# Layer borders taken one tile of 128 tokens at a time, and first feed-forward chunks with tokens on partitions

## The reference

```python
for layer in range(2):
    h = rms_norm(x, norm_mix_pre[layer])
    h = neighbourhood_attention(h, ...) if layer == 0 else dilated_attention(h, ...)
    x = x + rms_norm(h, norm_mix_post[layer])
    h = rms_norm(x, norm_ffn_pre[layer])
    x = x + rms_norm((silu(h @ w_gate) * (h @ w_up)) @ w_down, norm_ffn_post[layer])
for l in range(2):
    x = x + 0.5 * swiglu(rms_norm(x, ffn1_norm[l]), ...)
    x = x + hybrid_mixing(rms_norm(x, mix_norm[l]), ...) @ w_out[l]
    x = x + 0.5 * swiglu(rms_norm(x, ffn2_norm[l]), ...)
```

## Time and profile before

| | us |
|---|---|
| median of three runs (lowest, highest) | 1888.59 (1888.42, 1890.96) |
| the profiled execution's own time | 1888.44 |
| its span, first to last instruction | 1886.4 |
| TensorE matmuls busy | 1835.0 |
| VectorE, ScalarE, POOL busy | 1123.6, 899.5, 84.4 |
| HBM traffic over the span | 166 GB/s |
| mean granted clock of TensorE | 0.992 |

### The profile page before, as it was taken

One profiled execution on the slowest core, in us unless ns is written; L12 is line 12 of the kernel. 1 busy time (PEld: TensorE's weight loads), 2 busy tenths in 40 slices (PEclk: granted clock), 3 DMA queues, 4 the chain that ended last, 5 costly groups with the idle time before them and its releaser, 6 DMA issues.

```text
span 1886.4 us, 29866 instructions
## 1 busy us (share of the span) xinstructions
PE 1835.0 (97%) x12748; PEld 1682.5 (89%) x12748; DVE 1123.6 (60%) x1452; ACT 899.5 (48%) x1180; POOL 84.4 (4%) x157
## 2 busy tenths in 40 slices
PE   8989999899999899989999999999999999999999
PEld 6879998689998899889988888999899988889997
DVE  4765664446666566546654766665466547576663
ACT  5645443544444544444444654544454446445442
POOL 0000000202220000000000100000000001000000
PEclk9999999999999999999999999999999999999999
DMA  8433555453333355535554424545445544344452
GB/s 355 146 113 137 187 220 185 145 198 135 135 135 135 113 189 190 215 120 185 189 208 145 146 100 157 179 183 213 163 179 179 207 162 156 112 157 157 179 206 85
DMA packets 45091, 315.90 MB, mean 167 GB/s; under 512 B 5008, under 2 KB 5264, under 8 KB 7840
## 3 DMA queue, kind: packets, MB, share of 16 engines
q1 hardware_dynamic: 44928, 313.98, 45.8%
q0 software_dynamic: 32, 0.03, 0.0%
HBM read 312.94 MB, written 1.05 MB: 166 GB/s over the span
## 4 chain that ended last, share of the span: by engine, by line
PE 90%; DVE 4%; ACT 3%; issue 1%; POOL 1%; DMA 0%; SPq 0%; DVEq 0%; ACTq 0%
PE P L372 88%; DVE wl L1434 1%; ACT wh L983 1%; PE P L533 1%; PE P L385 1%; DVE hcv L1765 0%; DVE xl L1457 0%; ACT xh L1014 0%; POOL hsm L2048 0%; POOL nw L2001 0%; DVE hSS L1797 0%; ACT fs L1076 0%; DVE fg L1543 0%; DVE hxb L1760 0%; DVE rb L1466 0%
## 5 line engine op out<-in xcount | busy, mean ns | idle before, releaser
L1434 DVE TENSOR_TENSOR wl<-raw,wh 128x2048 fp32r<-128x2048 f32 x291 | 665.1, 2289 | 274.2 <-ACT wh L983 273.0
L372 PE MATMUL P<-xh,wh 128*128 128x256 f32 x2896 | 723.2, 287 | 8.3 <-DVE xl L1457 6.2
L372 PE MATMUL P<-xl,wh 128*128 128x256 f32 x2896 | 714.9, 284 | 0.0
L983 ACT ACTIVATE wh<-raw 128x2048 fp32r<-128x2048 f32 x291 | 553.1, 1902 | 238.3 <-PE P L372 231.3
L372 PEld LDWEIGHTS P<-xh,wh 128*128 128x128 f32 x2896 | 558.1, 193 | 19.8 <-issue 15.2
L372 PEld LDWEIGHTS P<-xl,wh 128*128 128x128 f32 x2896 | 558.5, 193 | 0.3
L372 PE MATMUL P<-xh,wl 128*128 128x256 f32 x2896 | 413.6, 284 | 1.9 <-DVE wl L1434 1.2
L372 PEld LDWEIGHTS P<-xh,wl 128*128 128x128 f32 x2896 | 376.9, 192 | 3.5 <-DVE wl L1434 3.5
L372 PE MATMUL P<-wh,fhl 128*128 128x512 f32 x528 | 207.9, 394 | 0.0
L372 PE MATMUL P<-wl,fhh 128*128 128x512 f32 x528 | 206.6, 391 | 0.0
L372 PE MATMUL P<-wh,fhh 128*128 128x512 f32 x528 | 205.7, 390 | 0.0
(11 more groups left out here) (289 smaller groups left out, 1349.5 us busy)
## 6 DMA issues: line engine op xcount, KB each, us to landing
raw<-w_all SPq DMA_DIRECT2D x290, 1024.0 KB, 4.8
nB<-rpb SPq DMA_DIRECT2D x4, 768.0 KB, 16.4
xs<-x_in SPq DMA_DIRECT2D x4, 256.0 KB, 5.1
fgb<-post SPq DMA_DIRECT2D x2, 512.0 KB, 6.3
raw<-w_all SPq DMA_DIRECT2D x2, 512.0 KB, 3.6
out<-xs SPq DMA_DIRECT2D x4, 256.0 KB, 2.1
C<-cst SPq DMA_DIRECT2D x1, 769.0 KB, 13.1
ngb<-post SPq DMA_DIRECT2D x1, 512.0 KB, 6.1
```

The costliest lines, as they stand in the source:

```text
L372: return t_.on.matmul(o, l, r, start=start, stop=stop, skip_group_check=True)
L983: a.on.activation(wh[k][:, 0:w], raw[r][:, 0:w], ACT.Copy).then_inc(*hi.up((m,)))
L1434: v.on.tensor_tensor(wl[k][:, 0:w], raw[r][:, 0:w], wh[k][:, 0:w].bitcast(F32), ALU.subtract).then_inc(*lo.up(m))
```

## The change

All borders are taken by tiles. `half` gets a parameter `split`: the last `split` pieces are used for tile 0 and then again for tile 1 (2 after the attentions, 3 after feed-forwards with post-norm, 1 elsewhere), and signals each tile. Post-norm, residual, `turn` (now 4 transposes of one tile t and one half q of the features), `xh` and `xl` (now 128 columns an instruction) are done tile by tile. The next step starts on tile 0 alone: `values_first` in the attentions and `gates_first` in steps 1, 3 and 4 use their first three pieces for tile 0, then for tile 1, with tile 1's turns between (`border`). In those three feed-forwards the first four chunks are computed with tokens on partitions, in two banks of gate and two of up; Silu and product follow per tile (`fth`), then 8 transposes (`gates_turn`, after chunk 4) bring them to the layout of the rest. The dilated attention keeps its tokens in their own order in `xh`; its second and third value projections read `xh` with a step of two tokens, and the q and k of all groups are put in order (even, odd) as they are read from PSUM. x is fetched tile 0 first. Below, 12 spaces of indentation are cut.

The plan of weight pieces and the constants:

```diff
 DOWN = [(k, h) for h in range(2) for k in range(NF)]
-LAST = [(k, 0) for k in range(6)] + [(k, 1) for k in range(4)] + [(6, 0), (7, 0)] + [(k, 1) for k in range(4, 8)]
+LAST = ([(k, 0) for k in range(6)] + [(k, 1) for k in range(2)] + [(k, 1) for k in range(2, 6)] +
+        [(6, 0), (7, 0), (6, 1), (7, 1)])
...
+        if tok:
+            for name in (g, u):
+                wide(name, layer, 8, 0, 512)
+        for j in range(4 if tok else 0, NF):
             out.append(("P", (g, layer, j * 128), (u, layer, j * 128)))
         halves(d, layer, DOWN)
...
-XBANK = {0: 6, 2: 7, 4: 6, 6: 7}
+TOK_FIRST = (1, 3, 4)
+BORDER = {1: (7, 9), 2: (3, 4), 3: (7, 9), 4: (7, 9)}
```

TensorE's program:

```diff
+def block(s, m, i, c, t, banks, names=(), perm=False):
...
+        o = P[b][:, :]
+        if c == 0:
+            claim(b)
+        mul(o, xa, h3[:, i, halfs(hf)], c == 0, False)
+        t_.wait_ge(*(lo.of(m, i) if m == 0 else lo.of(m)))
+        mul(o, xa, l3[:, i, halfs(hf)], False, False)
+        for z in ((0, 1) if perm else (t,)):
+            t_.wait_ge(*vx.of("lo", s, z, c))
+        k = mul(o, xb, h3[:, i, halfs(hf)], False, c == NK - 1)
+    if names:
+        k.then_inc(*mm.up(*names))
...
+def values_first(s, banks, start=None):
+    m = BASE[s]
+    for t in range(2):
+        for p in range(3):
+            for i in range(2):
+                block(s, m + p, i, 2 * p + i, t, banks[t], [("piece", m + p)] if t and i else ())
+                if t == 0:
+                    border(s, 2 * p + i)
+    tok(s, m + 3, 6, banks)
+def border(s, n):
+    if s and n == BORDER[s][0]:
+        turn(s, 1, 0)
+    if s and n == BORDER[s][1]:
+        turn(s, 1, 1)
+    if s == 0 and n == 1:
+        turn(0, 1, 0)
+        turn(0, 1, 1)
+def gates_first(s):
+    m = BASE[s]
+    place = [(0, 0), (0, 4), (1, 0), (1, 4)]
+    banks = ((0, 1), (2, 4))
+    def part(p, t):
+        g, c0 = place[p]
+        for i in range(4):
+            names = [("tok", s, g, t)] if p % 2 and i == 3 else []
+            if t and i == 3:
+                names.append(("piece", m + p))
+            block(s, m + p, i, c0 + i, t, (banks[g][t],), names)
+            if t == 0:
+                border(s, 4 * p + i)
+    for t in range(2):
+        for p in range(3):
+            part(p, t)
+    for t in range(2):
+        part(3, t)
+        held[banks[0][t]] = [(af, "ts", s, t)]
+        held[banks[1][t]] = [(vf, "th", s, t)]
...
+    whole = len(order) - 4 * split
...
+            if t == 1 and i % 4 == 3:
+                done.append(("piece", n))
...
-        m += 1
+    for i in range(whole):
+        rows(i, (0, 1))
+        after(i, 2)
+    for t in range(2):
+        for i in range(whole, len(order)):
+            rows(i, (t,))
+            after(i, t)
     for t in range(2):
...
+        if s in POST:
+            if t == 1 and i == 37:
+                turn(s + 1, 0, 0)
+            if t == 1 and i == 40:
+                turn(s + 1, 0, 1)
+        elif s < 9:
+            if i == 27:
+                turn(s + 1, 0, 0)
+                turn(s + 1, 1, 0)
+            if t == 1 and i == 41:
+                turn(s + 1, 0, 1)
...
+    if t == 1 and i == 13:
+        turn(s + 1, 0, 0)
+    if t == 1 and i == 15:
+        turn(s + 1, 0, 1)
...
-            next_turn(s)
+        if t == 0 and i == 14:
+            turn(s + 1, 0, 0)
+            turn(s + 1, 1, 0)
+        if t == 1 and i == 13:
+            turn(s + 1, 0, 1)
```

ScalarE's program (a.on):

```diff
+def post_end(s, banks):
+    m = BASE[s + 1]
+    if s in TOK_FIRST:
+        post_squares(s, 1, 0, banks)
+    else:
+        ahead(m)
+        post_squares(s, 0, 0, banks)
+        post_squares(s, 1, 0, banks)
+    post_root(s, 0)
+    ahead(m if s in TOK_FIRST else m + 1)
+    turn(s + 1, 0, 0)
+    turn(s + 1, 0, 1)
+    ahead(m + 1)
+    if s not in TOK_FIRST:
+        post_squares(s, 0, 1, banks)
+    post_squares(s, 1, 1, banks)
+    post_root(s, 1)
+    ahead(m + 2)
+    turn(s + 1, 1, 0)
+    turn(s + 1, 1, 1)
+    all_squares(s + 1)
...
+def add_end(s):
+    turn(s + 1, 0, 1)
+    squares(s + 1, 1, 0)
...
-    turn(0, 0)
-    turn(0, 2)
+    turn(0, 0, 0)
+    turn(0, 0, 1)
+    ahead(0)
+    turn(0, 1, 0)
+    turn(0, 1, 1)
     ahead(2)
-    turn(0, 4)
```

VectorE's program (v.on):

```diff
+def turn(s, t, q):
...
-        n = slice(j * S, (j + 1) * S)
-        k = v.on.scalar_tensor_tensor(lv[:, n], P[b][:, n], par(name, l, c + j), hv[:, n].bitcast(F32), ALU.mult,
-                                      ALU.subtract)
-    k.then_inc(*vx.up(("lo", s, c)))
-def factors(s):
+    v.wait_ge(*ax.of("hi", s, t, 4 * q + 3))
+    for j in range(4):
+        c = 4 * q + j
+        v.on.scalar_tensor_tensor(xl[:, c, toks(t)], P[b][:, toks(j)], par(name, l, c),
+                                  xh[:, c, toks(t)].bitcast(F32), ALU.mult,
+                                  ALU.subtract).then_inc(*vx.up(("lo", s, t, c)))
...
+def add(s, hf, t, banks, scale):
+    v.wait_ge(*mm.of("half", s, hf, t))
+    v.on.scalar_tensor_tensor(xs[:, t, halfs(hf)], P[banks[2 * hf + t]][:, :], scale, xs[:, t, halfs(hf)],
+                              ALU.mult, ALU.add).then_inc(*vx.up(("x", s, hf, t), ("free", s, hf, t)))
...
+def add_end(s, banks, scale):
+    add(s, 1, 0, banks, scale)
+    if s < 9:
+        turn(s + 1, 0, 1)
+    add(s, 1, 1, banks, scale)
...
+    v.wait_ge(*ax.of("psq", s, 1, t))
+    v.wait_ge(*vx.of("pre", s, t))
+    v.on.scalar_tensor_tensor(vv, ss[:, 10 + t:11 + t], 1.0 / D, ss[:, 12 + t:13 + t], ALU.mult,
+                              ALU.add).then_inc(*vx.up(("pv", s, t)))
+    gained(s, 1, t, gb, tmp, banks)
...
+    v.wait_ge(*ax.of("proot", s, t))
...
+def post_end(s, gb, tmp, banks):
+    m = BASE[s + 1]
+    if s not in TOK_FIRST:
+        ahead(m)
+        post_first(s, 0, gb, tmp, banks)
+    post_tile(s, 0, gb, tmp, banks)
+    ahead(m if s in TOK_FIRST else m + 1)
+    turn(s + 1, 0, 0)
+    turn(s + 1, 0, 1)
+    ahead(m + 1)
+    if s not in TOK_FIRST:
+        post_first(s, 1, gb, tmp, banks)
+    post_tile(s, 1, gb, tmp, banks)
+    ahead(m + 2)
+    turn(s + 1, 1, 0)
+    turn(s + 1, 1, 1)
...
 def na():
-    turn(0, 0)
-    turn(0, 2)
-    ahead(2)
-    turn(0, 4)
-    turn(0, 6)
-    for m in range(1, 4):
-        ahead(m + 2)
+    turn(0, 0, 0)
+    turn(0, 0, 1)
+    ahead(0)
...
-                               ALU.mult).then_inc(*va.up(("q", 2, f, z)))
+            qk, b = AD["dq"][:, (f % 3) * 3 + z, :], (3 * f + z) % 2
+            if z:
+                o = qk.rearrange("p (a t j) -> p a t j", a=2, t=2)
+                i = P[b][:, :].rearrange("p (a j t) -> p a t j", a=2, t=2)
+                r = far(rb[:, :]).unsqueeze(1).broadcast_to([128, 2, 2, 128])
+                v.on.tensor_tensor(o, i, r, ALU.mult).then_inc(*va.up(("q", 2, f, z)))
+            else:
+                v.on.tensor_tensor(near(qk[:, 0:S]), far(P[b][:, 0:S]), far(rb[:, :]), ALU.mult)
+                v.on.tensor_tensor(qk[:, S:2 * S], P[b][:, S:2 * S], rb[:, :],
+                                   ALU.mult).then_inc(*va.up(("q", 2, f, z)))
...
-    add(s, 0, banks, 1.0)
+    add_half(s, banks, 1.0)
     ahead(m + 20)
-    next_turn(s)
-    add(s, 1, banks, 1.0)
+    for t in range(2):
+        turn(s + 1, t, 0)
+    add_end(s, banks, 1.0)
```

More of the change, by code:

```diff
@@ new lines, in block, with tok @@
+                if names:
+                    k.then_inc(*mm.up(*names))
+            def tok(s, m, k0, banks, between=None, perm=False):
+                step = 4 // len(banks[0])
+                for i in range(step):
+                    for t in range(2):
+                        block(s, m, i, k0 + i, t, banks[t], [("piece", m)] if t and i == step - 1 else (), perm)
+                    if between is not None and i % 2 and k0 + i < NK - 1:
+                        between()
+            def values_first(s, banks, start=None):
[7 more added lines that the diff above has]
+                tok(s, m + 3, 6, banks)
@@ new lines, in half, with rows @@
+            def half(s, m, order, opnd, ready, banks, split, after):
+                last = {hf: max(i for i in range(len(order)) if order[i][1] == hf) for hf in range(2)}
+                first = {hf: min(i for i in range(len(order)) if order[i][1] == hf) for hf in range(2)}
+                whole = len(order) - 4 * split
+                def rows(i, ts):
+                    c, hf = order[i]
+                    n = m + i // 4
+                    ah_, al_ = opnd(c)
+                    t_.wait_ge(*hi.of(n))
+                    t_.wait_ge(*ready(c)[0])
+                    for t in ts:
+                        b = banks[2 * hf + t]
+                        o = P[b][:, :]
+                        if i == first[hf]:
+                            claim(b)
+                        mul(o, ah_[:, toks(t)], wh[n % RING][:, halfs(i % 4)], i == first[hf], False)
+                        t_.wait_ge(*lo.of(n))
+                        mul(o, ah_[:, toks(t)], wl[n % RING][:, halfs(i % 4)], False, False)
+                        t_.wait_ge(*ready(c)[1])
```

(28 more changed lines are left out.)

551 lines of the change are left out of this document (242 added, 309 removed).

## The result

The kernel after takes **1894.21 us** (median of 13 executions, 1890.96 to 1899.21), the kernel before 1888.79 beside it (13, 1887.19 to 1890.96): a ratio of **1.0028**, 95% interval 1.0019 to 1.0037. That is 5.4 us more, inside the range of 1880 to 1898 and 5.3 us over the forecast of 1888.9, so it falls just outside "no change". The profiled execution has a span of 1892.1 us.

The account below looks back on a forecast made before the run. TensorE was taken as the bound, its matmuls filling 97% of the span, so only its idle or slowed time counts. Terms -18.6 - 1.0 - 0.6 + 9.4 + 7.8 + 3.5 = +0.5 gave 1888.9 us, range 1880 to 1898.

Parts of the forecast that it names:

- (a): At the start, piece 1 is split behind tile 1's work: values 6.9 us later plus 2.5 of clock, +9.4 us.
- chunks: Chunks with tokens on partitions in three feed-forwards, fewer but wider matmuls plus 8 transposes: -0.3 us each, -1.0.
- (b): Out of the hybrids (5 to 6, 8 to 9), TensorE waits for tile 0's late addition: +3.9 us each, +7.8.
- (c): Out of feed-forwards without post-norm (4, 6, 7), TensorE waits 1.15 us for tile 0's addition: +3.5 us.
- The four borders: Borders behind post-norms (0 to 1 through 3 to 4): 35.1 us of idle and slow clock become 16.5 of stalls, gain 18.6.
- piece m+2: At the four borders, its `wl` comes behind tile 1's post-norm on VectorE: TensorE stalls 1.9 us each.
- Strided reads: Values 2 and 3 of the dilated attention, 192 loads with a step of two floats: taken as 0, upper 31 us.
- rival 1: Faster: the clock does not fall at the start and hybrids, 1882.4 us, or 1875 with m+2 stalls hidden; chance 0.31.
- Rival 2: Slower: late `wl` of m+2 makes the clock fall again at each of the four borders, 1897 us; chance 0.22.
- Rival 3: Slower: the strided loads in the dilated attention show, 1898 to 1919 us; chance 0.09.
- The slower side: Slower than before by over 0.2%, through Rival 2 or Rival 3: chance 0.22 + 0.09 = 0.31.

Follow-up runs that it names:

- e2: The kernel before with an unused tensor of 32 bytes per partition behind `rr`: 1895.35 us, ratio 1.0034 to before.
- e1: The kernel after with 32 unused bytes per partition behind `rp`: 1882.49 us, ratio 0.9962 to before.
- e5: The kernel before with an unused tensor of 64 bytes per partition behind `rr`: 1887.16 us, ratio 0.9991 to before.
- e3: e1 with the split of weight piece 1 moved ahead of ScalarE's and VectorE's work on the second tile at the start: 1880.99 us.
- e7: e3 plus, on VectorE behind hybrids and FFNs 4, 6, 7, the first tile's second-half addition before the next layer's second weight-piece split: 1869.59 us.
- e9: e7 with ScalarE splitting the fourth weight piece before its table load and VectorE the fifth before its products, before the tokens-first chunks: 1860.56 us.

## Why the prediction was right or wrong

Two pairs of kernels have equal places and so isolate the change. `after` against e2 gave -1.1 us in the medians. e1 (span 1879.5) against e5 (1884.5) gives **-5.0 us** (medians -4.7, or -5.3 by the ratios to before), with two short falls of the clock after 1100 us in each trace; the table takes this pair, as its traces hold equally many short falls. That the pairs differ by some 4 us is left open; two short falls of the clock would be 3.4, and the trace of `after` has three. By the first matmul of each projection, in the two traces:

| stretch | e5 | e1 | measured | predicted |
|---|---|---|---|---|
| up to the first output projection | 103.57 | 112.31 | +8.7 | (a) +9.4 |
| from there to the projection of FFN 4 | 853.87 | 834.82 | -19.0 | borders, chunks -19.6 |
| from there to the projection of FFN 9 | 863.05 | 868.98 | +5.9 | (b), (c) +11.3 |
| from there to the end | 64.1 | 63.4 | -0.7 | -0.6 |

- **The four borders**: right, with the mechanism. The idle for `xs` went, the clock stayed up, the stalls went over to `wl`. Those on piece m+2 are 1.28 to 1.32 us of idle each, the others 0.35 to 1.02, together 11.7 in e1. The forecast's 1.9 and 16.5 were counted from when TensorE would start the next matmul; counted so, from start to start, the ones on m+2 cost 1.65 to 1.68 and all fourteen 15.9. So the sum of the stalls was right within 0.6. Against it stand 1.2 us of strided loads and 0.8 of idle for `dV`, which I had at nothing.
- **(a)**: right. The values are read 9.2 us later, as TensorE waits 3.62 and 1.82 us (21.39, 23.71) and then runs at half clock; the new order of the splits and then the old start give it back.
- **(c)**: right, +1.1 and +1.25 us in the two FFNs (4, 6) whose stretches hold equal falls of the clock; 1.15 forecast.
- **(b)**: mechanism right, size wrong. I forecast +3.9 a hybrid. Between equally placed kernels it is +1.2 where the clock stays and +2.7 where it falls. The idle is 2.93 to 3.03 us, or 3.1 from start to start (1159.38 and one step of 0.23, to 1162.71), not 3.9. The addition ended 8.35 us after the first half's additions began (1154.21 to 1162.56), where 8.66 was forecast (1159.44 to 1168.1), as 128-column `xl` take 2.15 / 8 = 0.27 each and not 0.30. TensorE came to it after 5.4, not 4.8. Half of the term was a fall of the clock at each hybrid, which came in the trace of `after` at both and in that of e1 at one.
- **Strided reads**: the value taken, 0, was a little low. The chain in the values that read `xh` with a step of two floats, after, then the same values before:

```profile
379.79 10.27 PE P L387 x44
```

```profile
365.82 18.18 PE P L372 x80
```

233.4 against 227.3 ns, so 192 x 6.1 = 1.2 us, near the lower bound 0 and far from the 9.2 of the copy into `rb`, which was the wrong neighbour. By the rule of the Trainium skill ("Advanced Engine Details and Errata", Memory Cachelines) it would be 0 too; the traces show 1.2 us.

- **The step that failed** is the price of a 512-column matmul, 0.2275 taken from the chain of before and applied to the kernel after as well. `rp` was in the diff, and I costed it at nothing without naming it. It moved `fhh` from 64 to 32 bytes in front of `wh`'s place: 4.3 ns for some 1800 matmuls (1584 on `fhh` and `fhl`, the rest on `doh`, `dol` and the hybrids' `fce` group) = +7.8 us; the shift alone measured +5.7 (e2). In the traces the kernel after has three short falls of the clock behind 1100 us (1125, 1163, 1695), the kernel before one (1129). Such a fall lasts 3.4 us and costs half of it, so these two more are +3.4. With the -5.0 of the change at equal falls that makes 7.8 + 3.4 - 5.0 = +6.2, where the spans differ by 5.7 and the medians by 5.4.
- **The rivals**: rival 1 (the clock does not fall) is not what happened after: it fell at the start and behind both hybrids. Rival 2 did not happen: stalls of 1.3 us at the borders, clock 1.00. Rival 3 is 1.2 us, not 9. The slower side had 0.31, for reasons that did not come true; the reason that did was in none of them. That the forecast came near is luck: (b) and (c) together came out 5.4 us under their 11.3, (b) alone 3.9 under its 7.8, and the shift's 7.8 was missing, two errors against each other.

The version that beats both kernels is the change with `fhh` in the weights' place, the old start and the ends and pieces reordered: 1856.37 us, 1.7% under before, and 1855.73 with `noh` moved too.

## To carry to other kernels

Give stationary and moving operands of a matmul starts that are equal modulo 256 bytes, and look at addresses again whenever a tensor is added in front of them, however small; a step that changes in code that was not changed is the sign. This is measured for 512 columns of fp32r with a weight load per matmul. Splitting a border by tiles pays only if the step behind it can start on one tile. Count a wait from start to start, not by its idle (1.65 against 1.28 us here). And when work is put per tile, every queue has to be ordered for the first tile's next need: a split of a weight piece (2.3 us on VectorE) in front of a 0.7 us addition made a 3 us stall in front of the next turn.

## What the runs showed of the hardware

- The places of both operands set the step: with nothing else running, a 128 x 128 by 128 x 512 matmul steps at 226.7, 229 or 232.5 to 234.3 ns by the operands' relative address, while the loads' own records stay at 188 ns. The Trainium skill ("TensorE: Matmul & The Clock Gate", Step-by-step: what each phase is for) says that TensorE has two read ports into SBUF and that loading the next weights takes no read bandwidth from the running matmul; but a step that depends on where the two operands stand to each other, by up to 7.6 ns, does not fit two reads that never meet. The measurement decides; no run has matmuls without loads, so that it is the load that costs is not shown.
- Where the load reads with a step of two floats, the matmul's step is 6 ns longer too (233.4 against 227.3), and the load's own record goes from 188 to 193, before and then after:

```profile
L372 PEld LDWEIGHTS P<-wl,xh 128*128 128x128 f32 x79 | 14.8, 188 | 5.1 <-DVE wl L1434 2.1
```

```profile
L387 PEld LDWEIGHTS P<-wl,xh 128*128 128x128 f32 x75 | 14.4, 193 | 2.9
```

- The clock does not follow a single stall. Behind idles of 3.7 us it fell each time in the trace of before. Behind the 2.9 to 3.0 us at the first hybrid it fell in the trace of the kernel after and not in those of e1 and e3; with the same new start it fell in the trace of e7 and not in those of e3 and e9. One kernel's executions differ by it: e3 took 1874.3 us at a mean granted clock of 0.999 and 1880.9 to 1881.7 at 0.995 to 0.996.
